# Softmax probabilities written as a float16 and a bfloat16 part, and turned by two matmuls instead of one float32 transpose

## The reference

```python
sc = jnp.einsum('bqkgd,bskd->bkgqs', qb, kb).astype(jnp.float32) * scale
if rel_bias is not None:
    sc = sc + bias
...
p = jax.nn.softmax(sc, axis=-1)
o = jnp.einsum('bkgqs,bskd->bqkgd', p.astype(v.dtype), vb)
```

## Time and profile before

| | |
|---|---|
| time, median of 3 runs (lowest to highest) | 3417.04 us (3414.73 to 3417.45) |
| span of the profiled execution | 3411.3 us |
| PE busy | 3332.4 us, 98% |
| DVE busy | 1563.1 us, 46% |
| ACT busy | 961.5 us, 28% |
| POOL busy | 1543.4 us, 45% |
| chain that ended last, share on PE | 95% |

### The profile page before, as it was taken

How to read it: one execution, slowest core, us unless ns; L and a number is a source line. 1 busy time by engine, 2 the same in 40 slices (tenths; PEclk the granted TensorE clock), 3 DMA queues, 4 the chain that set the end, 5 groups by cost and what they waited for, 6 DMA issues and landing times.

```text
span 3411.3 us, 48542 instructions
## 1 busy us (share of the span) xinstructions
PE 3332.4 (98%) x19500; PEld 1699.2 (50%) x19500; DVE 1563.1 (46%) x2397; ACT 961.5 (28%) x1776; POOL 1543.4 (45%) x988
## 2 busy tenths in 40 slices
PE   8999998999999899999999999999999999999999
PEld 4555653655654344444445554555554444444444
DVE  4365558145547733332113366666566753333100
ACT  1434422233332400000002445555554410000000
POOL 4556762446664233333333566655665433333332
PEclk9999999999999999999999999999999999999999
DMA  3122112112111111111222011111112111111112
GB/s 130 40 52 61 58 61 96 44 44 70 49 67 34 43 50 49 49 51 50 70 69 89 29 58 52 52 55 46 52 35 93 54 44 49 49 51 54 46 51 82
DMA packets 55197, 194.28 MB, mean 57 GB/s; under 512 B 7408, under 2 KB 7792, under 8 KB 54512
## 3 DMA queue, kind: packets, MB, share of 16 engines
q1 hardware_dynamic: 52576, 182.96, 17.2%
q10 hardware_dynamic: 2448, 8.91, 0.7%
HBM read 172.97 MB, written 12.58 MB: 54 GB/s over the span
## 4 chain that ended last, share of the span: by engine, by line
PE 95%; DVE 2%; issue 1%; ACT 1%; POOL 1%; DMA 0%; DVEq 0%; POOLq 0%
PE pair L1078 27%; PE pair L1079 26%; PE pair L1080 26%; PE pair L1298 3%; PE pair L1267 3%; PE pair L1279 2%; PE pair L1471 1%; PE pair L1497 1%; PE pair L1482 1%; PE pair L1425 1%; PE pair L1098 1%; PE pair L1256 0%; DVE residual L1942 0%; DVE operand L1942 0%; ACT residual L1753 0%
## 5 line engine op out<-in xcount | busy, mean ns | idle before, releaser
L1078 PE MATMUL pair<-operand,panel_parts 128*128 128x512 f16 x2752 | 1049.1, 381 | 41.6 <-DVE operand L1942 26.2
L1079 PE MATMUL pair<-operand,panel_parts 128*128 128x512 bf16 x2752 | 1046.8, 380 | 0.0
L1080 PE MATMUL pair<-operand,panel_parts 128*128 128x512 f16 x2752 | 1046.4, 380 | 0.0
L883 POOL TENSOR_SCALAR panel_parts<-panel_raw 128x1024 f16<-128x1024 f32 (+3 forms) x280 | 285.7, 1020 | 1422.2 <-PE pair L1080 971.5
L884 POOL TENSOR_TENSOR panel_parts<-panel_raw,panel_parts 128x1024 bf16<-128x1024 f32 (+3 forms) x280 | 647.9, 2314 | 23.3
L1078 PEld LDWEIGHTS pair<-operand,panel_parts 128*128 128x128 f16 x2752 | 269.8, 98 | 386.3 <-issue 93.8
L1078 PE MATMUL pair<-arena,panel_parts 128*128 128x512 f16 (+2 forms) x1200 | 452.1, 377 | 8.7 <-issue 4.4
L920 POOL TENSOR_SCALAR arena<-arena,row_inv 128x256 f32<-128x256 f32 (+7 forms) x256 | 347.5, 1370 | 236.0 <-DVE row_inv L2008 235.6
L1080 PE MATMUL pair<-arena,panel_parts 128*128 128x512 f16 (+2 forms) x1200 | 451.3, 376 | 0.0
L1079 PE MATMUL pair<-arena,panel_parts 128*128 128x512 bf16 (+2 forms) x1200 | 451.3, 376 | 0.0
L1080 PEld LDWEIGHTS pair<-operand,panel_parts 128*128 128x128 bf16 x2752 | 270.1, 98 | 327.6 <-issue 4.9
(11 more groups left out here) (219 smaller groups left out, 3955.3 us busy)
## 6 DMA issues: line engine op xcount, KB each, us to landing
panel_raw<-in_wgu SPq DMA_DIRECT2D x88, 512.0 KB, 3.5
panel_raw<-in_wl SPq DMA_DIRECT2D x58, 512.0 KB, 3.6
panel_raw<-in_wm SPq DMA_DIRECT2D x56, 512.0 KB, 3.6
panel_raw<-in_wdn SPq DMA_DIRECT2D x32, 512.0 KB, 3.6
residual<-residual_spill SPq DMA_DIRECT2D x15, 512.0 KB, 6.2
panel_raw<-in_wl SPq DMA_DIRECT2D x18, 384.0 KB, 3.1
panel_raw<-in_wdn SPq DMA_DIRECT2D x16, 384.0 KB, 3.1
residual<-in_xT ACTq DMA_DIRECT2D x8, 512.0 KB, 11.3
```

What stands on the lines that cost most here:

```text
L883: chained(nc.gpsimd.tensor_scalar(hi[:, c], RAW[:, s, c], HI_MAX, -HI_MAX, ALU.min, ALU.max))
L1078: nc.tensor.matmul(out, stat[0], mov[0], start=first, stop=False)
L1079: nc.tensor.matmul(out, stat[0], mov[1], start=False, stop=False)
L1080: return nc.tensor.matmul(out, stat[1], mov[0], start=False, stop=last)
```

## The change

POOL's `scale` is removed, in the layers and in the mixer. In its place ACT writes the product of a unit's probabilities and their inverse sums in float16 (`slot_scale_hi`, mixer `scale_hi`: a copy with a scale, into the new tile `probs_hi`), and DVE writes the same product in float32 minus that float16 part, in bfloat16 (`slot_scale_lo`, mixer `scale_lo`, into `probs_lo`). PE turns each block by two matmuls that add up in the same PSUM block, with the part as weights and a float16 identity as the moving operand. The identity is made once by ACT. `dynamic_dma_scratch_size=1024` is set at the kernel's creation; no transfer is started by POOL.

```diff
-            def scale(n, group):
-                _, s = SLOTS[n]
-                pool.wait_ge(slot_inverse, 2 * n + group + 1)
-                for u in s.groups[group]:
-                    p = probs_of(n, s, u)
-                    b = 4 * (n % 2) + u.i
-                    nc.gpsimd.tensor_scalar(p, p, RI[:, b:b + 1], None, ALU.mult).then_inc(slot_scaled, 1)
...
-                            if part == (2 if s.branch == "c" else 1):
-                                scale(n + 1, 0)
...
                     for x, (i, j) in enumerate(blocks):
-                        p = probs_of(n, s, s.units[i])
-                        m = nc.tensor.transpose(TRB[b][:, x * P:(x + 1) * P], p[:, j * P:(j + 1) * P], ident[:])
+                        hi, lo = probs_parts(n, s, s.units[i])
+                        k = slice(j * P, (j + 1) * P)
+                        nc.tensor.matmul(TRB[b][:, x * P:(x + 1) * P], hi[:, k], ident16[:], start=True, stop=False)
+                        m = nc.tensor.matmul(TRB[b][:, x * P:(x + 1) * P], lo[:, k], ident16[:], start=False, stop=True)
...
+            def slot_scale_hi(n, g):
+                _, s = SLOTS[n]
+                act.wait_ge(slot_inverse, 2 * n + g + 1)
+                for u in s.groups[g]:
+                    b = 4 * (n % 2) + u.i
+                    copy(probs_parts(n, s, u)[0], probs_of(n, s, u), RI[:, b:b + 1]).then_inc(slot_scaled_hi, 1)
...
                         if not gate_first:
                             keep_layer((l, s.n, part))
+                        if nxt and part == (2 if s.branch == "c" else 1):
+                            slot_scale_hi(n + 1, 0)
+                            if nxt != "b":
+                                slot_scale_hi(n + 1, 1)
+                        if part == 3 and nxt == "b":
+                            slot_scale_hi(n + 1, 1)
...
                         if part == 1:
                             keep_turned(n, 0)
                             keep_turned(n, 1)
+                        if part == 2 and n + 1 < MIX_TURNS * TT:
+                            scale_hi(n + 1)
                         keep((j, p, part))
...
+            def slot_scale_lo(n, g):
+                _, s = SLOTS[n]
+                for u in s.groups[g]:
+                    b = 4 * (n % 2) + u.i
+                    hi, lo = probs_parts(n, s, u)
+                    dve.wait_ge(slot_scaled_hi, PROBS_AT[n, u.i])
+                    stt(lo, probs_of(n, s, u), RI[:, b:b + 1], hi, ALU.mult, ALU.subtract).then_inc(slot_scaled, 1)
...
                     keep_layer((l, s.n, 2))
+                    if nxt and s.branch != "c":
+                        slot_scale_lo(n + 1, 0)
+                        if nxt != "b":
+                            slot_scale_lo(n + 1, 1)
                     layer_background(l, s, 2)
...
                         slot_gate(n)
                         layer_background(l, s, 3)
+                        if nxt == "b":
+                            slot_scale_lo(n + 1, 1)
                         continue
...
+            def scale_lo(n):
+                for h in range(2):
+                    b = 2 * (n % 2) + h
+                    hi, lo = mix_parts(n, h)
+                    dve.wait_ge(mix_scaled_hi, 2 * n + h + 1)
+                    stt(lo, mix_probs_at(n, h), RI[:, b:b + 1], hi, ALU.mult, ALU.subtract).then_inc(mix_scaled, 1)
...
                     gate(n)
                     if more:
+                        scale_lo(n + 1)
                         keep_dense((j, p, 3))
                     background(j, p, 3)
```

More of the change, by code:

```diff
@@ L413, in build @@
         row_mean = sb("row_mean", [P, 4])
+        ident16 = sb("ident_half", [P, P], HI)
+        PH = sb("probs_hi", [P, 2, 2 * T], HI)
+        PL = sb("probs_lo", [P, 2, 2 * T], LO)
         zero = RC[:, 3:4]
@@ L514, in build @@
         slot_scaled = sem("slot_scaled")
+        slot_scaled_hi = sem("slot_scaled_hi")
+        ident_half_ready = sem("ident_half_ready")
         slot_turned = [sem(f"slot_turned{b}") for b in range(2)]
@@ L648, in probs_of, with probs_parts @@
             return PB[n % 2][:, u.i * w:u.i * w + u.nk]
+        def probs_parts(n, s, u):
+            c0 = u.h * T if s.branch == "b" else u.i * (640 if s.branch == "a" else 256)
+            return PH[:, n % 2, c0:c0 + u.nk], PL[:, n % 2, c0:c0 + u.nk]
         def bias_of(s, u):
@@ L696, in mix_probs_at, with mix_parts @@
             return PBM[2 * (n % 2) + h][:, 0:MIX_UNITS[n % TT].nk]
+        def mix_parts(n, h):
+            c = slice(h * HALF, h * HALF + MIX_UNITS[n % TT].nk)
+            return PH[:, n % 2, c], PL[:, n % 2, c]
         def piece_ready(engine, piece):
@@ L943, in _ @@
                 follow((l, -1, 0))
-                for g in range(2):
-                    scale(l * NSLOT, g)
                 for s in LAYER_SLOTS:
-                    n = l * NSLOT + s.n
                     for part in range(4):
-                        if s.n + 1 < NSLOT:
-                            if part == (2 if s.branch == "c" else 1):
-                                scale(n + 1, 0)
[L952 to L955, removed]
                         follow((l, s.n, part))
@@ L1026, in bias @@
                 m.then_inc(mix_bias_ready, 1)
[L1028 to L1033, removed]
             def follow(at):
@@ L1046, in _ @@
                     bias(0)
-            scale(0)
             for j in range(MIX_TURNS):
                 for p in range(TT):
-                    n = j * TT + p
                     for part in range(4):
-                        if part == 1 and n + 1 < MIX_TURNS * TT:
-                            scale(n + 1)
                         if (p, part) == (1, 1) and j + 1 < MIX_TURNS:
@@ L1479, in mix_turn @@
                     pe.wait_ge(mix_kept, 2 * n + h - 1)
+                hi, lo = mix_parts(n, h)
                 for x in range(MIX_UNITS[n % TT].ne):
                     w = slice(x * P, (x + 1) * P)
-                    m = nc.tensor.transpose(TRB[h][:, w], mix_probs_at(n, h)[:, w], ident[:])
+                    nc.tensor.matmul(TRB[h][:, w], hi[:, w], ident16[:], start=True, stop=False)
+                    m = nc.tensor.matmul(TRB[h][:, w], lo[:, w], ident16[:], start=False, stop=True)
                 m.then_inc(mix_turned, 1)
@@ L1707, in _ @@
                 slot_exponents(l * NSLOT, 0)
+                if l == 0:
+                    act.wait_ge(const_loaded, 16 * 6)
+                    copy(ident16[:], ident[:]).then_inc(ident_half_ready, 1)
+                for g in range(2):
+                    slot_scale_hi(l * NSLOT, g)
                 pos = kept_at(l, "bkv")
@@ L1857, in exponents, with scale_hi @@
                                          accum_out=RS[:, b:b + 1]).then_inc(mix_probs, 1)
+            def scale_hi(n):
+                act.wait_ge(mix_inverse, n + 1)
+                for h in range(2):
+                    b = 2 * (n % 2) + h
+                    copy(mix_parts(n, h)[0], mix_probs_at(n, h), RI[:, b:b + 1]).then_inc(mix_scaled_hi, 1)
             def keep_turned(n, h):
@@ L2253, in _ @@
                     slot_invert(first, g)
+                for g in range(2):
+                    slot_scale_lo(first, g)
                 for s in LAYER_SLOTS:
@@ L2287, in _ @@
                     keep_layer((l, s.n, 3))
+                    if s.branch == "c":
+                        slot_scale_lo(n + 1, 0)
+                        if nxt != "b":
+                            slot_scale_lo(n + 1, 1)
                     layer_background(l, s, 3)
+                    if nxt == "b":
+                        slot_scale_lo(n + 1, 1)
                 dve.wait_ge(slot_gated, first + NSLOT)
@@ L2611, in _ @@
             invert(0)
+            scale_lo(0)
             for j in range(MIX_TURNS):
```

5 lines of the change are left out of this document (4 added, 1 removed).

## The result

The changed kernel takes 3476.16 us (median of 4 runs, 3474.01 to 3478.71), against 3416.19 us for the kernel before measured beside it: ratio 1.0175, 95% interval 1.0161 to 1.0190, so 60 us slower. The forecast was 3428, with a range up to 3441. The direction was right, the size was not: five times the +11 of the sum.

What follows compares the result with a forecast made beforehand. PE, busy 98% of the span, was taken as the bound. Terms 2.7 + 2.1 + 4.9 + 1.6 + 2.0 - 2.2 = +11.1 us, on the median of 3417.04, gave 3428 us; range 3413 to 3441.

Steps and rivals of the forecast that it cites:

- PE's own work: PE's turns in layers and mixer: 1128 transposes at 109 ns become 2256 matmuls at 55.9 ns, +2.7 us.
- Relief: Branch b of each layer and the mixer's start: PE's waits for POOL held by scales go, -2.2 us.
- Gate pieces: Mixer turns: ACT's two copies between the first and second gate piece make PE wait, 8 x 0.62 = +4.9 us.
- DVE beside POOL ... I take 0: DVE operation stretched to 3.04 us beside POOL's split at 361.66: split would move earlier, so 0; otherwise +4.4 us.
- The collision rival: DVE and POOL still collide, in layers and once or twice in the mixer: up to +9 us, 3432 to 3437; chance 0.14.
- the prediction's own signs of being wrong: PE idle elsewhere in slots until DVE's rest, turn matmuls at 80 ns or more, or 1.2 us DVE operations taking 3.
- Smaller places: Branch a, the change b to m, and branch c: short stalls, +1.0 us a layer, +2.0 us in all.
- The wait of branch b that was worked out as 1.0 us: Branch b, 1024 to 896 keys: late row maximum delays PE's next scores 1.0 us a layer, +2.1 us in all.
- Turn 7: Mixer, turn 7: DVE is behind, and the rests make PE's turn of step 57 late, +1.6 us.

Runs made afterwards that it cites:

- The fills: POOL's second split instruction replaced by two fills of the same columns, in the changed kernel (3422.71 us) and in the kernel before (3402.12 us).
- 3378 us: Kernel before, with POOL's scale writing the probabilities in float16 and one float16 matmul for a block, rest left out: 3377.72 us, ratio 0.9882.

## Why the prediction was wrong

**PE's own work: right.** +2.7 us, 56 ns a matmul, in every kernel with two of them. With the rests left out, all that the prediction named beside them (2.7 for PE, 4.9 for the gate pieces, -2.2 for POOL's waits) sums to +5.4; measured is +6.4. This sum's 4.9 for the gate pieces was written as 8 x 0.62, while the text above it had worked out 0.64, which makes 5.1.

**Relief: right.** The matmuls near 371 no longer wait; the same loads come 1.1 us closer together there, in both layers, and 0.6 at the mixer's start.

**Gate pieces: right in place and size.** This is the first of them, in the changed kernel, with PE's use of the bank of the earlier trace rows:

```profile
1986.25 1.11 ACT L1578 ACTIVATE probs_hi<-arena,row_inv 128x384 f16<-128x384 f32 x2
...
1987.99 0.39 PE L1065 MATMUL pair<-arena,panel_parts 128*128 128x512 f16 x1 [0.45 <-ACT arena L1830]
```

Moving the copies away gave 0.62 us a turn; 0.64 were forecast, for eight turns, and seven have it.

**The step that failed: "DVE beside POOL ... I take 0".** The row was there: 3.04 us for 1.22 beside a split. At that one place the argument held: the split came earlier (368.93, about 359 on the clock of before), and the old operation took 1.22 us again, at 372.72. But the prediction used the row for one old operation at one place, and priced every new rest, 384 of them, as if alone. Two things were missed. A rest meets a split wherever POOL happens to be, and pays what is left of it: in branch b 2.70 us and 4.36 for two, in the mixer 3.44 for two of 256 columns. And POOL without scales doesn't only end earlier, it moves: its bias sum and its splits now stand beside other DVE operations. At the very place of the earlier trace rows the split that had moved out of the old operation's way met a rest of 512 columns, which took 2.21 us. The fills show 39 us of the 60 for this, and the step that hangs on the moved bias sum is about 10 of it. Part of the 39 is the clock, by the last section: at most 8.5 us, by estimate. The collision rival stood at 0.14 and +9: right in kind, four times too small. Two of the prediction's own signs of being wrong came as written: PE idle in the slots until a rest is done, and DVE operations of 1.2 us still taking 3.

**"Smaller places", +2.0: too small.** With fills in both kernels the distance is 20.6, not 11. The wait of branch b that was worked out as 1.0 us is 0.75 there, so that term was right for rests that no split stretches. The step of 1.6 us a layer at the first slot of branch b was not seen at all: two rests of 1024 columns before one row maximum, 2.5 us of DVE in front of a slack that held 0.7 elsewhere. The others are of the size read, but there are five a layer.

**Turn 7: right in place, not in cause.** PE waited 2.42 us for the rest of step 57, where 1.6 were taken for the rests' own length. With fills the same turn has no listed wait and a step of 0.5, so most of it is stretching; a 1024-wide DVE operation of 2.26 us beside a split stands ahead of it:

```profile
2655.40 2.26 DVE L1961 TENSOR_TENSOR arena<-arena 128x1024 f32<-128x1024 f32 x1 [1.94 <-ACT arena L1859]
...
2660.75 0.29 PE L1473 MATMUL pair<-ident_half,probs_hi 128*128 128x128 f16 x1 [2.42 <-DVE probs_lo L1964]
```

**ACT's queue behind a late row maximum: missed.** The prediction followed a late row maximum to PE's next scores only. In the mixer the longer way is the dear one: exponentials, and the copy of a dense piece behind them.

What stays open: how the 39 us divide among rests that are stretched, older operations that the moved splits stretch, and the clock; which places make up the 10 us that the sum lacks with fills; and what bounds the layers at 3378 us.

## What to carry to other kernels

Work that is moved to VectorE with two SBUF operands has to be priced with GpSimd's longest neighbour added wherever the two can meet, not at its time alone; the slacks of 0.3 to 0.7 us in this schedule are smaller than one such meeting. Taking work off GpSimd moves all that stands behind it, and each of those operations meets new neighbours: compare where they land before counting the relief. Several causes can share one wait, so what each edit gives back may not be added to what another gives. And for a turn that may be rounded, one float16 matmul for a block costs half of a float32 transpose (56 against 109 ns); the two matmuls of this change cost as much as the transpose, so they had nothing to win on PE.

## What the runs showed of the hardware that was not expected

A VectorE operation with two SBUF operands that starts beside GpSimd's two-operand split ends about its own time after the split's end: 2.70 us for 1.2 at 397.29. Beside a GpSimd fill, which reads nothing, the same operation took 1.28. Beside the old scales, which read one tensor from SBUF, such an operation took 1.28 too (211.25 in the kernel before), so the scales were the milder neighbour there. The Trainium skill (SBUF — State Buffer, Who interferes with whom) has both halves, the exclusive lock and that such an operation is held only by a GpSimd operation that reads SBUF; the rows with the split and with the fill agree with both, the one beside the scales shows hardly any hold.

After four of the long waits PE's matmuls ran at a granted clock of 0.50, the 1.2 GHz level, and the starts of 128-column matmuls lay some 106 ns apart: behind 2.59 us at 216.33 and again at 789.51, 2.16 at 974.22, and 2.42 at 2660.75. Behind 2.16 us at 401.06 and 2.42 at 336.77 the clock stayed at its upper level, 2.4 GHz, and the distances at 56 ns. What tells the two kinds apart these runs don't show. Windows, the clock behind the busy times:

```profile
216.00:220.00 4.00, 3.67 (x35) 3.38 (x36) 4.00 (x6) 0.00 (x0) 0.00 (x0) 0.57 0.33 119
...
401.00:404.40 3.40, 3.35 (x24) 1.96 (x25) 2.15 (x6) 3.28 (x6) 0.00 (x0) 1.00 0.03 11
...
974.20:981.00 6.80, 6.78 (x25) 3.79 (x26) 3.51 (x7) 4.16 (x7) 0.00 (x0) 0.50 0.02 8
...
2660.70:2662.00 1.30, 1.25 (x12) 1.25 (x13) 1.30 (x3) 0.14 (x1) 0.00 (x0) 0.50 0.00 0
```

The place at 974 is that of 401 in the other layer, with the same wait. It cost 4.8 us by the same loads, the one at 401 cost 2.6: the difference of 2.2 us is the clock's. Over the four places the share of the clock that was withheld, times the length, is 8.5 us in this execution, as an estimate from above. The kernel before has none of the four, and neither has the changed kernel with fills; the kernel before has one at 2710 (0.97 over the 60 us from 2700, so 1.8 us) that the changed kernel lacks.
